# Six of a feed-forward block's first products taken from the stream not yet normalised, with eight PSUM banks in turn

## The chip, the cores and the metric

The kernel runs on one core of one Trainium2 chip. Its time is the device time of one execution in microseconds (us), lower is better; a kernel's figure is the median of its runs. TensorE does the matrix products into PSUM (8 banks of 512 float32 columns in each of 128 partitions), VectorE (DVE) and ScalarE (ACT) do the elementwise work, SyncE issues nearly all loads, GpSimd (POOL) a few subtractions.

## What is computed

The reference runs two stacks on 256 tokens of width 1024. The first (a conditioned block of attention with low-rank projections, short convolution and mixtures of experts) ends in an RMS norm. The change touches only the second stack, which is two layers of

```
x = layer_norm(ALPHA * x + 0.5 * swiglu_ffn(x, ffn1_w_gu, ffn1_w_down))
x = layer_norm(ALPHA * x + hybrid_mixer(x, w_in, w_out, ...))
x = layer_norm(ALPHA * x + 0.5 * swiglu_ffn(x, ffn2_w_gu, ffn2_w_down))

def swiglu_ffn(x, w_gu, w_down):
    a, u = split(x @ w_gu)          # 1024 -> 2 * 2816
    return (silu(a) * u) @ w_down   # 2816 -> 1024
```

All values are float32. The kernel gets float32 accuracy from fp32r products: a factor is split into a high part (rounded to fp32r) and a low part (the rest), and high*high + high*low + low*high are added up in PSUM.

## The kernel before

**Order of work.** Each engine runs its own program, written out stage by stage in Python; the order inside an engine is the order in which the methods `pe`, `act`, `dve`, `pool` of the stage classes issue instructions, and the engines meet through counting semaphores (`L.wait`, `L.inc`). Nothing reorders it. The stages of a layer are `ffns[0]`, `lns[0]`, `mixer`, `lns[1]`, `ffns[1]`, `lns[2]`, and two layers follow each other.

**Units of weight.** A feed-forward block (`Ffn`) first computes 22 pairs of 128 hidden features: unit 2f is the gate part, unit 2f+1 the linear part of pair f, and a unit is 128 columns of `w_gu` over all 8 tiles of 128 inputs. The weights of a unit are cast by ACT (`round_weights`, L2374, 128x1024) to the high part and subtracted by DVE (`split_weights`, L2379) to the low part, in one of `UNITS` = 4 buffers in `WS`; unit u can be cast only when unit u-4 has been multiplied (`units_used`). The loads from memory run ahead into `ring`.

**Two forms of a unit.** From unit `RAW_UNITS` = 4 on, `products` (L2398, L2403) multiplies the unit with the normalised stream, whose high and low parts lie in `XS`: 8 times a product of 512 columns (high weights with both parts of x) and one of 256. ACT then copies one half out of PSUM (`keep_low`, L2444) and DVE adds the other (`sum_parts`, L2503). The first four units are "raw" (`raw_products`, L587 to L589): they multiply the stream as it is before the norm is known, times the norm's gain (`RAW_HIGH`, `RAW_LOW`), 24 products of 260 or 256 columns. Once the norm's mean and reciprocal root are known, DVE corrects them in three steps (`correct_raw`, L595, L597, L600). DVE then forms silu(a)*u (L2525 or L2528) and splits it for the second matrix (`split_hidden`, L2510).

**The entries.** There are four places where a norm leads into a feed-forward block, and at each TensorE works on raw units while DVE and ACT finish the norm. Entry 1 is `norms[4]` (class `Norm`) into `ffns[0]` of the first layer; entries 2 and 4 are `lns[1]` (class `LayerNorm`, after the mixer) into `ffns[1]` of the first and second layer; entry 3 is `lns[2]` (class `EarlyLayerNorm`) into `ffns[0]` of the second layer. At entries 2 and 4 TensorE's order is unit 0, the sums of squares (`pe_sums`, L1034), a wait for the variance, units 1 to 3, then unit 4 as the pieces of `XS` appear (`stream_high` L780 on ACT, `stream_low` L784 on DVE). In `LayerNorm` ACT squares (L1056), casts unit 4, takes the root (L1060), then adds the bias (L1063) and casts to `XS` tile by tile; DVE subtracts the mean, splits units 2 and 3, adds epsilon to the variance (L1080), splits unit 4, takes the reciprocal (L1083), scales the tiles (L1086) and splits unit 5 last.

**PSUM.** Pairs f use banks 0/1, 2/3, 4/5 in turn (`bank`), so that unit u >= 6 waits until pair u//2-3 is finished (`hidden`). The norm's sums lie in banks 2 and 3 (`LayerNorm`) or 6 and 7.

## Time and profile before

| | |
|---|---|
| time, median of 3 runs | 2259.85 us (2259.22 to 2265.28) |
| the profiled execution: its time, its span | 2261.75 us, 2259.9 us |
| TensorE busy | 1980.1 us, 88% of the span |
| DVE busy, ACT busy | 1203.0 us (53%), 795.0 us (35%) |
| granted TensorE clock, mean | 0.955 of full speed |

The span runs from the first to the last instruction; the execution's time lies 1.85 us above it. The second stack begins at about 1222 us of the span. In the timeline a row is start, duration, engine, line, operation, output<-inputs, shapes and count; a bracket tells how long the engine sat idle and who released it. Matmul ends are modelled, so pace is read from start to start.

### The profile page before, as it was taken

Reading aid. Unit: us, or ns where it says so; the run is one execution under the profiler, and the core shown is the slowest. Engines: PE = TensorE matmul, PEld = TensorE weight load, DVE = VectorE, ACT = ScalarE, POOL = GpSimd, SP = SyncE. Lnnn points to the kernel's source line nnn. Section 1 sums busy time; section 2 is a strip of 40 time slices with the busy share of each in tenths; the row PEclk is TensorE's granted clock in tenths of the full one; section 3 lists DMA queues with packets and bytes.
Section 4 is the critical chain, followed back from the end, with each engine's and each line's share of the span. In section 5 each row is a group of like instructions: output and inputs, shape, how many; then the busy total and the mean of one; then the engine's idle time right before and its main releaser. Section 6 shows DMA issues by size and latency. Waiting matters only on the chain.

```text
span 2259.9 us, 45225 instructions
## 1 busy us (share of the span) xinstructions
PE 1980.1 (88%) x17666; PEld 1533.0 (68%) x17669; DVE 1203.0 (53%) x2486; ACT 795.0 (35%) x1535; POOL 28.3 (1%) x39
## 2 busy tenths in 40 slices
PE   7989887766779988766677999998999999998998
PEld 3557554434449855443445888987888888987887
DVE  3798322111227632111124766877767766877766
ACT  2233110000014411000003654555655654556554
POOL 0000000000000000000000000100001000100000
PEclk9999999888989999888898999999999999999999
DMA  9779999999997699999999645416656545416651
GB/s 409 299 320 392 429 431 431 432 431 431 431 431 301 253 393 431 432 432 432 431 432 400 219 145 184 161 48 214 203 150 221 177 149 179 162 49 223 203 150 59
DMA packets 238736, 660.83 MB, mean 292 GB/s; under 512 B 6416, under 2 KB 197920, under 8 KB 208672
## 3 DMA queue, kind: packets, MB, share of 16 engines
q1 hardware_dynamic: 238160, 657.25, 73.8%
q10 hardware_dynamic: 464, 2.05, 0.2%
q8 instruction: 75, 1.23, 0.2%
q14 instruction: 37, 0.30, 0.0%
HBM read 658.22 MB, written 1.06 MB: 292 GB/s over the span
## 4 chain that ended last, share of the span: by engine, by line
PE 60%; DMA 21%; DVE 11%; SPq 3%; issue 2%; ACT 2%; another core or an unknown queue 1%; PEld 0%; DVEq 0%; ACTq 0%; PEldq 0%
PE ps L2398 19%; PE ps L2403 10%; DMA A<-in_moe_w_up 8%; PE ps L1748 7%; DMA ring<-in_moe_w_up 6%; DMA arena<-in_moe_w_up 4%; PE ps L2730 3%; PE ps L1777 3%; SPq L3296 2%; DVE ring L546 2%; DMA ring<-in_ffn_w_gu 2%; PE ps L2886 2%; PE ps L1730 1%; PE ps L1698 1%; PE ps L2180 1%
## 5 line engine op out<-in xcount | busy, mean ns | idle before, releaser
L2398 PE MATMUL ps<-XS,WS 128*128 128x512 f32 x1280 | 449.8, 396 | 8.3 <-DVE WS L2379 8.2
L2379 DVE TENSOR_TENSOR WS<-ring,WS 128x1024 fp32r<-128x1024 f32 (+1 forms) x272 | 324.0, 1193 | 176.5 <-ACT WS L2374 176.0
L2374 ACT CAST WS<-ring 128x1024 fp32r<-128x1024 f32 (+1 forms) x272 | 278.3, 1024 | 275.8 <-PE ps L2403 258.9
L2403 PE MATMUL ps<-XS,WS 128*128 128x256 f32 x1280 | 357.9, 280 | 0.0
L2028 DVE TENSOR_TENSOR RS<-RS,ps 64x256 f32<-64x256 f32 x70 | 29.6, 423 | 577.7 <-ACT RS L1837 577.7
L1748 PE MATMUL ps<-ring,RS 128*32 128x256 f32 x2176 | 238.8, 451 | 87.2 <-DMA ring<-in_moe_w_up 32.6
L2398 PEld LDWEIGHTS ps<-XS,WS 128*128 128x128 f32 x1280 | 240.1, 188 | 68.1 <-issue 6.1
L2403 PEld LDWEIGHTS ps<-XS,WS 128*128 128x128 f32 x1280 | 241.4, 189 | 0.0
L1748 PEld LDWEIGHTS ps<-ring,RS 128*32 128x32 f32 x2176 | 127.2, 129 | 149.6 <-issue 128.8
L2398 PE MATMUL ps<-HS,WS 128*128 128x512 f32 x616 | 216.4, 396 | 0.0
L1748 PE MATMUL ps<-arena,RS 128*32 128x256 f32 x1120 | 168.3, 467 | 49.9 <-DMA A<-in_moe_w_up 24.9
L1837 ACT ACTIVATE RS<-ps 64x256 f32<-64x256 f32 x70 | 26.3, 375 | 487.8 <-PE ps L1748 487.8
L2403 PE MATMUL ps<-HS,WS 128*128 128x256 f32 x704 | 197.0, 280 | 0.0
L1748 PEld LDWEIGHTS ps<-arena,RS 128*32 128x32 f32 x1120 | 82.7, 134 | 86.8 <-issue 76.7
L2398 PEld LDWEIGHTS ps<-HS,WS 128*128 128x128 f32 x616 | 115.5, 188 | 27.3
L2403 PEld LDWEIGHTS ps<-HS,WS 128*128 128x128 f32 x704 | 133.0, 189 | 0.1
L1748 PE MATMUL ps<-SPARE,RS 128*32 128x256 f32 x576 | 81.5, 446 | 47.3 <-DMA arena<-in_moe_w_up 24.0
L1843 ACT COPY arena<-ps 128x256 f32<-128x256 f32 x70 | 26.0, 372 | 266.4 <-PE ps L1777 266.4
L546 DVE CUSTOM_DVE_ANT_0 ring<-ring,arena,VECS 128x1024 f32<-128x1024 f32 x80 | 98.8, 1280 | 4.8 <-DMA ring<-in_mod_later 4.7
L1748 PEld LDWEIGHTS ps<-SPARE,RS 128*32 128x32 f32 x576 | 45.1, 128 | 79.4 <-issue 68.2
L2034 DVE COPY arena<-ps 64x128 f32<-64x128 f32 x140 | 39.7, 283 | 105.4 <-PE ps L1764 103.2
L1748 PE MATMUL ps<-A,RS 128*32 128x256 f32 x608 | 85.9, 446 | 0.0
(410 smaller groups left out, 3526.7 us busy)
## 6 DMA issues: line engine op xcount, KB each, us to landing
ring<-in_ffn_w_gu SPq DMA_DIRECT2D x88, 1024.0 KB, 7.4
arena<-in_moe_w_down SPq DMA_DIRECT2D x32, 2048.0 KB, 48.7
ring<-in_moe_w_up SPq DMA_DIRECT2D x32, 2048.0 KB, 47.8
ring<-in_moe_w_down SPq DMA_DIRECT2D x32, 2048.0 KB, 47.7
ring<-in_moe_w_gate SPq DMA_DIRECT2D x32, 2048.0 KB, 46.5
ring<-in_ffn_w_down SPq DMA_DIRECT2D x32, 1408.0 KB, 6.4
ring<-in_mod_later SPq DMA_DIRECT2D x20, 2048.0 KB, 10.6
SPARE<-in_moe_w_gate SPq DMA_DIRECT2D x16, 2048.0 KB, 43.5
```

Of the source, the lines that this page charges most:

```text
L546: L.inc(L.eng.tensor_tensor_reduce(out=rows, in0=rows, in1=COND_ROW, scale=1.0, scalar=vcol("b_mod", 1, 48 * l + c), op0=ALU.mult, op1=ALU ...
L1748: mm = pe.matmul(ps[self.lane_rows(q), 0, 0:HALF_FF], x, weight, start=k == 0, stop=k == KD - 1)
L1777: mm = pe.matmul(ps[self.lane_rows(q), 7, 0:D // 4], self.HB[:, c, :], down[:, c, q * (D // 4):(q + 1) * (D // 4)], start=c == 0, stop=c = ...
L2028: v.tensor_tensor(self.H[0:2 * CAP], self.SG[2 * CAP:P], ps[2 * CAP:P, 0, 0:HALF_FF], ALU.mult)\
L2034: v.tensor_copy(self.HB[h * 2 * CAP:(h + 1) * 2 * CAP], turned[:, h]).then_inc(self.h_kept.sem, 1)
L2374: L.inc(L.eng.copy(self.parts(u)[0], source), self.w_high)
L2379: L.inc(L.eng.tensor_tensor(wl, self.unit(u)[1], high(wh), ALU.subtract), self.w_split)
L2398: L.eng.matmul(ps[:, bank, :].rearrange("p (j t) -> p j t", j=2), wh[:, i, :], moving[:, :, k, :], start=k == 0, stop=False)
L2403: mm = L.eng.matmul(ps[:, bank, 0:TL], wl[:, i, :], moving[:, 0, k, :], start=False, stop=k == total - 1)
L2730: mm = pe.matmul(out_ap, weights[:, k, :], XS[:, x, k, :], start=k == 0 and x == 0 and weights is high_part, stop=k == KD - 1 and weights ...
L2886: mm = pe.matmul(self.y_tile(m), weights[:, k - first, cols], YS[:, k, x, :], start=m % 2 == 0 and k == 0 and x == 0 and weights is high_part,
L3296: sp.dma_start(loads[at][0][0], src).then_inc(slot_in[place_of[at]].sem, 16)
```

## The change

Units 4 and 5 become raw as well (`RAW_UNITS` 6), so the stream of `XS` is first needed at unit 6. Eight banks are used in turn, beginning at bank 4 where a `LayerNorm` precedes; the wait for the variance moves from unit 2 to unit 6, and the wait for a finished pair now reaches back four pairs. The casts and splits of units 5, 6 and 7 move into the norm: unit 5 goes into its middle, units 6 and 7 to its end (they were done inside pair 1 of the feed-forward block). Units 4 and 5 need DVE's three correction steps instead of an ACT copy and one DVE addition.

In `LayerNorm` the cast of unit 5 stands ahead of ACT's wait for the variance, in `Norm` and `EarlyLayerNorm` behind the root.

```diff
--- before.py
+++ after.py
@@ -72,7 +72,7 @@
 UNITS = (RING - RING_2) * SLOT // (2 * UNIT)
 MIXER_UNITS = 4 * 5 + KD
 CONV_AHEAD = 2
-RAW_UNITS = 4
+RAW_UNITS = 6
 FFN_UNITS = 2 * FFT + KD * 3
 FIRST_BYTE = SCRATCH + 256
 
@@ -694,10 +694,12 @@
                                            bias=LNP[:, (2 * self.i + 1) * KD + k:(2 * self.i + 1) * KD + k + 1]), self.done)
                     if k and on:
                         stream_high(L, self.done, k - 1, self.split)
+                    if k == 3 and on and stage is ffns[0]:
+                        stage.round_weights(L, UNITS + 1, later)
                 if on:
                     stream_high(L, self.done, KD - 1, self.split)
-                    if self.raw:
-                        stage.round_weights(L, UNITS + 1, later)
+                    for u in (2, 3) if stage is ffns[0] else (1,):
+                        stage.round_weights(L, UNITS + u, later)
                 end(L, "act")
 
             def dve_first(self, L, k):
@@ -752,11 +754,13 @@
                         stream_low(L, k - 2, self.split)
                     if k == 3 and on and self.raw:
                         stage.split_weights(L, UNITS, later)
+                    if k == 6 and on and stage is ffns[0]:
+                        stage.split_weights(L, UNITS + 1, later)
                 if on:
                     for k in (KD - 2, KD - 1):
                         stream_low(L, k, self.split)
-                if on:
-                    stage.split_weights(L, UNITS + 1, later)
+                    for u in (2, 3) if stage is ffns[0] else (1,):
+                        stage.split_weights(L, UNITS + u, later)
                 end(L, "dve")
 
             def pool(self, L):
@@ -957,9 +961,11 @@
                         L.inc(L.eng.activation(CONV_XS[:, 0, k, :], A[:, k, 0:T], ACT.Identity, bias=self.shift(k)), conv.x_high)
                     conv.round_weights(L, CONV_AHEAD)
                 else:
+                    ffns[0].round_weights(L, UNITS + 1)
                     for k in range(KD):
                         stream_high(L, self.scaled, k, self.split)
-                    ffns[0].round_weights(L, UNITS + 1)
+                    for u in (UNITS + 2, UNITS + 3):
+                        ffns[0].round_weights(L, u)
                 end(L, "act")
 
             def dve(self, L):
@@ -988,6 +994,8 @@
                                                          op0=ALU.mult, op1=ALU.mult), self.scaled)
                         if k >= 2:
                             stream_low(L, k - 2, self.split)
+                        if k == 4:
+                            ffns[0].split_weights(L, UNITS + 1)
                 if self is norms[2]:
                     for k in range(KD):
                         L.eng.wait_ge(conv.x_high.sem, k + 1)
@@ -997,7 +1005,8 @@
                 if self.which == 2:
                     for k in (KD - 2, KD - 1):
                         stream_low(L, k, self.split)
-                    ffns[0].split_weights(L, UNITS + 1)
+                    for u in (UNITS + 2, UNITS + 3):
+                        ffns[0].split_weights(L, u)
                 end(L, "dve")
 
 
@@ -1055,7 +1064,8 @@
                     L.wait(self.centred, k + 1)
                     L.inc(L.eng.activation(LN_TILES[:, k, TL:TA], LN_TILES[:, k, 0:TL], ACT.Square), self.squares)
                 stage, later = self.next
-                stage.round_weights(L, UNITS, later)
+                for u in (UNITS, UNITS + 1):
+                    stage.round_weights(L, u, later)
                 L.wait(self.var, 1)
                 L.inc(L.eng.activation(RS[:, 0, 0:TL], RS[:, 0, 0:TL], ACT.Sqrt), self.std)
                 for k in range(KD):
@@ -1065,7 +1075,8 @@
                     if k:
                         stream_high(L, self.done, k - 1, self.split)
                 stream_high(L, self.done, KD - 1, self.split)
-                stage.round_weights(L, UNITS + 1, later)
+                for u in (UNITS + 2, UNITS + 3):
+                    stage.round_weights(L, u, later)
                 end(L, "act")
 
             def dve(self, L):
@@ -1073,12 +1084,12 @@
                 for k in range(KD):
                     L.inc(L.eng.tensor_tensor(LN_TILES[:, k, 0:TL], XT[:, k, 0:TL], LN_MEAN, ALU.subtract), self.centred)
                 stage, later = self.next
-                stage.split_weights(L, UNITS - 2, later)
-                stage.split_weights(L, UNITS - 1, later)
+                for u in (UNITS - 2, UNITS - 1, UNITS):
+                    stage.split_weights(L, u, later)
                 L.wait(self.sums, 1)
 
                 L.inc(L.eng.tensor_scalar(RS[:, 0, 0:TL], ps[:, self.banks[1], 0:TL], LN_EPS / ALPHA ** 2, None, ALU.add), self.var)
-                stage.split_weights(L, UNITS, later)
+                stage.split_weights(L, UNITS + 1, later)
                 L.wait(self.std, 1)
                 L.inc(L.eng.reciprocal(RS[:, 0, 0:TL], RS[:, 0, 0:TL]))
                 L.join()
@@ -1090,7 +1101,8 @@
                         stream_low(L, k - 2, self.split)
                 for k in (KD - 2, KD - 1):
                     stream_low(L, k, self.split)
-                stage.split_weights(L, UNITS + 1, later)
+                for u in (UNITS + 2, UNITS + 3):
+                    stage.split_weights(L, u, later)
                 end(L, "dve")
 
 
@@ -2380,7 +2392,7 @@
 
             def bank(self, u):
 
-                return 2 * (u // 2 % 3) + u % 2
+                return 2 * ((u // 2 + (2 if self.entry else 0)) % 4) + u % 2
 
             def pe(self, L):
 
@@ -2404,9 +2416,6 @@
                     L.inc(mm, self.w_used)
 
                 for u in range(RAW_UNITS):
-                    if u == 2 and self.entry:
-                        L.wait(self.entry.var, 1)
-                        L.wait(self.entry.mean_kept, 1)
                     raw_products(L, self, u, self.bank(u))
                     if u == 0 and self.entry:
                         self.entry.pe_sums(L)
@@ -2415,8 +2424,11 @@
                         L.eng.wait_ge(stages_done.sem, norms[4].before_sums)
                         L.eng.sem_inc(stages_done.sem, 1)
                 for u in range(RAW_UNITS, 2 * FFT):
-                    if u >= 6:
-                        L.wait(self.hidden, u // 2 - 2)
+                    if u == RAW_UNITS and self.entry:
+                        L.wait(self.entry.var, 1)
+                        L.wait(self.entry.mean_kept, 1)
+                    if u >= 8:
+                        L.wait(self.hidden, u // 2 - 3)
                     products(u, self.bank(u), XS)
                 L.wait(self.hidden, FFT - 1)
                 for m in range(KD):
@@ -2445,13 +2457,14 @@
 
                 for f in range(FFT):
                     raw = 2 * f < RAW_UNITS
-                    if f:
+                    if f > 1:
                         round_weights(UNITS + 2 * f)
                     if not raw:
                         L.wait(self.hidden, f - 1)
                         keep_low(2 * f, SA[f % 2], self.bank(2 * f), self.low_kept)
                     if f:
                         round_hidden(f - 1)
+                    if f > 1:
                         round_weights(UNITS + 2 * f + 1)
                     L.wait(self.summed, f + 1)
                     if raw:
@@ -2512,11 +2525,12 @@
                 for f in range(FFT):
                     raw = 2 * f < RAW_UNITS
                     part = correct if raw else sum_parts
-                    if f:
+                    if f > 1:
                         split_weights(UNITS + 2 * f)
                     part(2 * f, SA[f % 2], self.summed)
                     if f:
                         split_hidden(f - 1)
+                    if f > 1:
                         split_weights(UNITS + 2 * f + 1)
                     part(2 * f + 1, HF[f % 2])
                     L.wait(self.silu, f + 1)
```

**ACT inside `LayerNorm`, from the squares (L1056, now L1065) to the second tile of the scaled stream.** `WS` is the weight buffer, `RS` holds the root; the waits are `split_used` (an earlier unit has been multiplied), `norm_var` (variance ready), `norm_scaled` (a tile scaled by DVE). Before:

```order
L1056 ACTIVATE arena<-arena 128x256 [waits ln_centred] x8
L2374 CAST WS<-ring 128x1024 [waits split_used,slot_in2]
L1060 ACTIVATE RS<-RS 128x256 [waits norm_var]
L1063 ACTIVATE XT<-XT,LNP 128x256 [waits norm_scaled] x2
L780 CAST XS<-XT 128x256 [waits norm_done]
```

Now:

```order
L1065 ACTIVATE arena<-arena 128x256 [waits ln_centred] x8
L2386 CAST WS<-ring 128x1024 [waits split_used,slot_in2] x2
L1070 ACTIVATE RS<-RS 128x256 [waits norm_var]
L1073 ACTIVATE XT<-XT,LNP 128x256 [waits norm_scaled] x2
L784 CAST XS<-XT 128x256 [waits norm_done]
```

There are two casts (units 4 and 5) ahead of the root where there was one.

**DVE inside `LayerNorm`, from the centring (L1074, now L1085) to the reciprocal.** L1080 (now L1091) reads the sum of squares, L2379 (now L2391) is a split. Before:

```order
L1074 TENSOR_TENSOR arena<-XT,RS 128x256 x7
L2379 TENSOR_TENSOR WS<-ring,WS 128x1024 [waits split_high] x2
L1080 TENSOR_SCALAR RS<-ps 128x256 [waits norm_sums]
L2379 TENSOR_TENSOR WS<-ring,WS 128x1024 [waits split_high]
L1083 RECIPROCAL RS<-RS 128x256 [waits norm_std]
```

Now:

```order
L1085 TENSOR_TENSOR arena<-XT,RS 128x256 x7
L2391 TENSOR_TENSOR WS<-ring,WS 128x1024 [waits split_high] x3
L1091 TENSOR_SCALAR RS<-ps 128x256 [waits norm_sums]
L2391 TENSOR_TENSOR WS<-ring,WS 128x1024 [waits split_high]
L1094 RECIPROCAL RS<-RS 128x256 [waits norm_std]
```

Unit 4 is split ahead of the variance, and unit 5 in the place that unit 4 had.

**DVE at the start of the feed-forward block, from the first product with silu (L2525, now L2539) to the split of unit 8.** L595, L597 and L600 are one correction, L2510 (now L2523) is `split_hidden`. Before:

```order
L2525 SCALAR_TENSOR_TENSOR arena<-arena,SPARE 128x256 [waits loop_line_dve,ffn_silu]
L2379 TENSOR_TENSOR WS<-ring,WS 128x1024 [waits split_high]
L595 TENSOR_REDUCE SPARE<-ps 128x2 [waits split_used]
L597 SCALAR_TENSOR_TENSOR arena<-RS,SPARE,ps 128x256 [waits loop_line_dve]
L600 TENSOR_TENSOR arena<-arena,RS 128x256 [waits loop_line_dve]
L2510 TENSOR_TENSOR HS<-arena,HS 128x256 [waits ffn_h_high]
L2379 TENSOR_TENSOR WS<-ring,WS 128x1024 [waits split_high]
L595 TENSOR_REDUCE SPARE<-ps 128x2 [waits split_used]
L597 SCALAR_TENSOR_TENSOR arena<-RS,SPARE,ps 128x256 [waits loop_line_dve]
L600 TENSOR_TENSOR arena<-arena,RS 128x256 [waits loop_line_dve]
L2525 SCALAR_TENSOR_TENSOR arena<-arena,SPARE 128x256 [waits loop_line_dve,ffn_silu]
L2379 TENSOR_TENSOR WS<-ring,WS 128x1024 [waits split_high]
```

Now:

```order
L2539 SCALAR_TENSOR_TENSOR arena<-arena,SPARE 128x256 [waits loop_line_dve,ffn_silu]
L595 TENSOR_REDUCE SPARE<-ps 128x2 [waits split_used]
L597 SCALAR_TENSOR_TENSOR arena<-RS,SPARE,ps 128x256 [waits loop_line_dve]
L600 TENSOR_TENSOR arena<-arena,RS 128x256 [waits loop_line_dve]
L2523 TENSOR_TENSOR HS<-arena,HS 128x256 [waits ffn_h_high]
L595 TENSOR_REDUCE SPARE<-ps 128x2 [waits split_used]
L597 SCALAR_TENSOR_TENSOR arena<-RS,SPARE,ps 128x256 [waits loop_line_dve]
L600 TENSOR_TENSOR arena<-arena,RS 128x256 [waits loop_line_dve]
L2539 SCALAR_TENSOR_TENSOR arena<-arena,SPARE 128x256 [waits loop_line_dve,ffn_silu]
L2391 TENSOR_TENSOR WS<-ring,WS 128x1024 [waits split_high]
```

The splits of units 6 and 7 are gone from between the corrections; they stand, with nothing between them, at the norm's end, where the split of unit 5 stood. The split of unit 8 closes the same list of DVE work in both.

## Rows read from the trace of the kernel before

**Rows 1.** The page: span, and busy time of each engine.

```profile
span 2259.9 us, 45225 instructions
PE 1980.1 (88%) x17666; PEld 1533.0 (68%) x17669; DVE 1203.0 (53%) x2486; ACT 795.0 (35%) x1535; POOL 28.3 (1%) x39
```

**Rows 2.** Waits of TensorE, 1225 to 2260: total us, times, longest.

```profile
PE ps L2398 <- DVE WS L2379: 8.2, 7, 1.5
```

**Rows 3.** Timeline of TensorE at entry 2: units 0, 1, 5, 6, 8.

```profile
1550.05 0.28 PE L589 MATMUL ps<-RAW_HIGH,WS 128*128 128x260 f32 x1
...
1556.35 0.28 PE L589 MATMUL ps<-RAW_HIGH,WS 128*128 128x260 f32 x1
...
1566.45 0.50 PE L2398 MATMUL ps<-XS,WS 128*128 128x512 f32 x1 [1.09 <-DVE WS L2379]
...
1570.61 0.47 PE L2398 MATMUL ps<-XS,WS 128*128 128x512 f32 x1 [1.11 <-DVE WS L2379]
...
1576.23 0.39 PE L2398 MATMUL ps<-XS,WS 128*128 128x512 f32 x1
```

**Rows 4.** Timeline of DVE at entry 2: splits, reciprocal, first corrections.

```profile
1554.16 1.22 DVE L2379 TENSOR_TENSOR WS<-ring,WS 128x1024 fp32r<-128x1024 f32 x1
1555.29 1.75 DVE L1083 RECIPROCAL RS<-RS 128x256 f32<-128x256 f32 x1
...
1565.17 1.23 DVE L2379 TENSOR_TENSOR WS<-ring,WS 128x1024 fp32r<-128x1024 f32 x1 [0.49 <-ACT WS L2374]
1566.54 0.16 DVE L595 TENSOR_REDUCE SPARE<-ps 128x2 f32<-128x4 f32 x1
...
1569.24 1.22 DVE L2379 TENSOR_TENSOR WS<-ring,WS 128x1024 fp32r<-128x1024 f32 x1
...
1571.76 1.22 DVE L2379 TENSOR_TENSOR WS<-ring,WS 128x1024 fp32r<-128x1024 f32 x1
...
1574.54 1.22 DVE L2379 TENSOR_TENSOR WS<-ring,WS 128x1024 fp32r<-128x1024 f32 x1
```

**Rows 5.** Timeline of ACT at entry 2: casts of units 4 and 5, the root.

```profile
1550.42 1.05 ACT L2374 CAST WS<-ring 128x1024 fp32r<-128x1024 f32 x1 [0.71 <-PE ps L589]
1554.28 0.42 ACT L1060 ACTIVATE RS<-RS 128x256 f32<-128x256 f32 x1 [2.81 <-DVE RS L1080]
...
1564.10 1.04 ACT L2374 CAST WS<-ring 128x1024 fp32r<-128x1024 f32 x1
```

**Rows 6.** Timeline of DVE and TensorE at entry 1: unit 8 split, unit 8 begun.

```profile
1254.75 1.22 DVE L2379 TENSOR_TENSOR WS<-ring,WS 128x1024 fp32r<-128x1024 f32 x1
...
1256.55 0.40 PE L2398 MATMUL ps<-XS,WS 128*128 128x512 f32 x1
```

**Rows 7.** The same of entry 3.

```profile
1764.69 1.22 DVE L2379 TENSOR_TENSOR WS<-ring,WS 128x1024 fp32r<-128x1024 f32 x1
...
1766.49 0.40 PE L2398 MATMUL ps<-XS,WS 128*128 128x512 f32 x1
```

**Rows 8.** Timeline at entry 4: reciprocal, unit 1's last product, unit 8.

```profile
2063.87 1.75 DVE L1083 RECIPROCAL RS<-RS 128x256 f32<-128x256 f32 x1
...
2064.93 0.28 PE L589 MATMUL ps<-RAW_HIGH,WS 128*128 128x260 f32 x1
...
2083.11 1.22 DVE L2379 TENSOR_TENSOR WS<-ring,WS 128x1024 fp32r<-128x1024 f32 x1
...
2084.81 0.39 PE L2398 MATMUL ps<-XS,WS 128*128 128x512 f32 x1
```

**Rows 9.** Windows: length, busy PE, PEld, DVE, ACT, POOL, granted clock, DMA.

```profile
1542.00:1544.00 2.00, 1.13 (x4) 0.68 (x4) 1.42 (x4) 1.76 (x3) 0.00 (x0) 1.00 1.09 386
1544.00:1546.00 2.00, 1.68 (x4) 0.90 (x4) 1.15 (x3) 1.19 (x4) 0.00 (x0) 0.68 0.96 341
1546.00:1548.00 2.00, 1.55 (x8) 1.53 (x8) 1.51 (x5) 1.42 (x5) 0.00 (x0) 0.50 0.04 16
...
1568.00:1570.00 2.00, 1.50 (x9) 1.05 (x8) 1.85 (x4) 1.80 (x4) 0.00 (x0) 1.00 0.00 0
...
2054.00:2056.00 2.00, 1.31 (x5) 0.89 (x6) 1.26 (x4) 1.44 (x4) 0.00 (x0) 1.00 0.96 341
```

More of the change, by code:

```diff
@@ L152 @@
 ACT_PER_LAYER = 7
-DVE_PER_LAYER = 172
-DVE_LAST = 169
+DVE_PER_LAYER = 180
+DVE_LAST = 177
 SPLITS_PER_LAYER = 2 * FFN_UNITS + MIXER_UNITS
```

## The prediction

> **What bounds the kernel now.** I read the page first. TensorE is busy for 1980.1 of 2259.9 us [rows 1], and in the second stack nearly without a break, so a change there can only give back what TensorE waits for. The waits of TensorE say how much that is: for a split of weight units 5 to 7 it sat idle 7 times, 8.2 us in total and never over 1.5 us at once [rows 2]. Each of these lies at one of the four entries, one at entry 1 and two at each of the others. That is the whole purse: 8.2 us of 2259.9, or 0.36%. About 0.3% is what a measurement of this kernel can tell from no change.
>
> The timelines of one entry say why it waits there. At entry 2 TensorE begins unit 6 at 1570.61 after 1.11 us of idleness, released by DVE's split that began at 1569.24 [rows 3, 4]. From the start of a split to the first product of its unit is 1570.61 - 1569.24 = 1.37 us. DVE itself hardly rests between the reciprocal at 1555.29 and the split of unit 8 at 1574.54 [rows 4]. So at the entries DVE's list of work is the bound. By unit 8 it is no longer: the split at 1574.54 would let unit 8 begin at 1575.91, and TensorE comes only at 1576.23 [rows 3, 4], 0.32 late. That slack is the same kind at the other entries: 1254.75 + 1.37 = 1256.12 against 1256.55, so 0.43 [rows 6]; 1764.69 + 1.37 against 1766.49, 0.43 [rows 7]; 2083.11 + 1.37 against 2084.81, 0.33 [rows 8].
>
> **The change part by part.** *Raw units 4 and 5 on TensorE* cost nothing: by their columns a raw unit (8 times 260 + 256 + 260) is 1% more than a unit on `XS` (8 times 512 + 256), and units 6 and 7 need (1576.23 - 1570.61) / 2 = 2.81 us each from start to start [rows 3], so a raw one 2.84. What is won is that they need no `XS`, so TensorE can run them while the norm ends.
>
> *The splits of units 6 and 7* move ahead of the first two pairs' corrections. TensorE then doesn't wait for them behind corrections; it waits for unit 8 instead. This is the step that decides the sum. Ahead of the split of unit 8 DVE has the same list as before: the splits up to unit 7, the corrections of units 0 to 3, two products with silu, one split of hidden values. Only the order within the list differs, as the excerpt of DVE's order shows. So unit 8 can't be split earlier than before unless DVE's idle time shrinks. Then each entry gains no more than its slack, as TensorE, now ahead of time, takes unit 8 as soon as it is split. At entries 1 and 3 I take just that: -0.43 and -0.43. The inner split of unit 5 there (behind the third or fifth tile of the stream) delays the rest of the stream by one split, 1555.29 - 1554.16 = 1.13 us [rows 4], which is the split that vanished from the end.
>
> *The cast of unit 5 ahead of the root* (entries 2 and 4) is what adds a wait. It needs unit 1 to have been multiplied. TensorE starts unit 1 only behind the sums of squares; its last product begins at 1556.35 [rows 3]. After unit 0 the cast began 1550.42 - 1550.05 = 0.37 later [rows 3, 5], so unit 5 is cast from 1556.72. ACT's root stood at 1554.28 [rows 5] and is now behind it. DVE's split of unit 5 follows its cast by 1565.17 - 1564.10 = 1.07 [rows 4, 5], so from 1557.79, and it too stands ahead of the reciprocal, which comes 1.13 later: 1558.92 instead of 1555.29. The norm is 3.63 late. Entry 4 gives the same: unit 1's last product at 2064.93 puts the reciprocal at 2064.93 + 0.37 + 1.07 + 1.13 = 2067.50, against 2063.87, again 3.63 [rows 8]. Queued behind are the scaling of eight tiles, their casts, the casts and splits of units 6 and 7 and all corrections. One split (1.13) of the list has been done inside the delay, so unit 8 is split 3.63 - 1.13 = 2.50 later than before; less the slack, TensorE begins it 2.18 late at entry 2 and 2.17 at entry 4.
>
> What TensorE sees at entry 2: units 2 to 5 follow unit 1 without a break, 1556.35 + 4 x 2.84 = about 1567.8; unit 6 can be split at 1564.10 + 3.63 + 1.07 = 1568.80 and begins at 1570.17, after 2.3 us of waiting; unit 8 begins at 1576.23 + 2.18 = 1578.41, after another 2.6. Two waits of 1.1 idle have become two of over 2.
>
> The trace shows first that a ready root can stand behind a cast: at 1550.42 ACT sat 0.71 for TensorE with its next work queued behind [rows 5]. The Trainium skill, "TensorE: Matmul & The Clock Gate", section "Architectural detail: the array is 16× 32×32, not 1× 128×128", calls the queues of ScalarE and VectorE strictly first in, first out, which speaks against this change; by it the two entries lose 2.2 us each, and if either engine could pass the waiting pair they would gain their slack. The trace agrees so far as the one wait of 0.71 shows.
>
> *Eight banks and the later waits* cost nothing and give nothing. The wait for a pair four back instead of three would matter if TensorE waited for finished pairs; among its waits from 1225 on, only the splits of units and the edges of the mixer appear, and the former make 8.2 us [rows 2]. The wait for the variance moves to unit 6, which needs the finished stream anyway. If that cover were gone it would be the same moment: the stream needs the root.
>
> *Two more corrections per entry* on DVE (units 4 and 5) replace two ACT copies and two DVE additions. Behind the split of unit 8 the splits must now come every 2.81. A split, a correction, a split of hidden values and the next split take 1571.76 - 1569.24 = 2.52; a split, a correction, a product with silu and the next split 1574.54 - 1571.76 = 2.78 [rows 4]. So unit 9 is ready 0.29 ahead of TensorE and unit 10 0.32 ahead: no new wait, but the cover is thin. Without it each unit costs what it lacks; I take zero, at most 0.5 per entry.
>
> *Sum*: -0.43 + 2.18 - 0.43 + 2.17 = +3.5 us. It stands against the profiled execution, 2261.75 with a span of 2259.9; that lies 1.9 above the median of 2259.85, so I carry the difference over: 2259.85 + 3.5 = **2263.3 us**, 0.15% slower, which a measurement calls no change.
>
> **The rivals.** *The clock falls in the new waits* (slower side of the same mechanism). At entry 2 the trace has a stretch in which TensorE worked 1.13 and 1.68 of 2 us, and the granted clock fell to 0.68 and then 0.50, the level of 1.2 GHz [rows 9]; the like stretch at entry 4 kept 1.00 with 1.31 of 2 busy, and so did the present waits at 1.50 of 2 [rows 9]. With two waits of over 2 us around one unit the new stretch has about as little work as the one that fell. The fall in the rows cost 1.68 x 0.32 + 1.55 x 0.50 = 1.3 us of TensorE's busy time, and a whole unit at half pace would cost 2.8; I take 1.7, nearer to the row. One fall gives 2265, three give 2268.4. For it: idle shares like those before the fall. Against: DVE still bounds unit 8, so slow units 6 and 7 would be hidden. The Trainium skill, same page, section "A second HAM failure mode: psum-queue depth-cycling", says that short idle times between groups of matmuls can make the clock swing between its two levels; by that page entries 2 and 4 would fall each time, about 2266.7 by the price above. The trace has both outcomes for like stretches. Chance 0.25.
>
> *The block at entries 2 and 4 doesn't bite* (other side). If the cast of unit 5 is ready before the root (unit 1 done sooner, or the sums later), the reciprocal stays, and all four entries gain their slack: -0.43 - 0.32 - 0.43 - 0.33 = -1.5, 2258.3. The point that decides is whether unit 1 ends before the variance; now it ends 2.1 us behind the root's start (1556.35 against 1554.28) [rows 3, 5], and nothing in the change moves it forward. Chance 0.12.
>
> *The waits vanish as meant*: if DVE has reserve that I don't see and unit 8 comes early too, up to 8.2 us of idleness goes [rows 2], 2251.7, the only way to faster by over 0.3%. DVE's nearly unbroken row from 1555.29 to 1574.54 speaks against it [rows 4]. Chance 0.05.
>
> *DVE falls behind in pairs 2 and 3*: 0.5 per entry on top, 2265.3. Chance 0.08. My forecast as it stands: 0.50.
>
> **How the numbers follow.** Within the forecast the handovers may each be off by some tenths, 2261.5 to 2265.1. The range takes in the rival without the block at its lower end and two or three falls of the clock at its upper: 2257.5 to 2269.5; the full success and many falls stay out. Faster by over 0.3% (below 2253.1) is the vanishing alone, 0.05. Slower by over 0.3% (above 2266.6) needs two falls or a fall with DVE behind: most of the clock's 0.25 and some of the rest of the cases, less what is hidden, 0.19. That leaves 0.76 within 0.3%.
>
> **What would show it.** Right: at entries 2 and 4 ACT's root starts about 3.4 us later, behind a cast that waited for TensorE; the reciprocal 3.6 later; TensorE waits over 2 us before unit 6 and again before unit 8; at entries 1 and 3 a wait before unit 8 alone, and unit 8 0.4 nearer to the entry's start. Wrong: a reciprocal in its old place, unit 8 reached without a wait, waits from unit 9 on, or a granted clock under 1.00 behind an entry.

## The result, and the profile after

The changed kernel takes 2265.03 us (median of 20 runs, 2261.74 to 2270.72), the kernel before in the same comparison 2262.10 us (20 runs, 2258.50 to 2265.85). The ratio is **1.0018, 95% interval 1.0011 to 1.0024**: slower by 0.18%, which is within the 0.3% that counts as no change. On the first median of before the ratio gives 2259.85 x 1.0018 = 2263.9 us; the prediction was 2263.3.

The page of the profiled execution (2261.74 us) shows almost no difference to before [rows 1]:

```profile
span 2259.8 us, 45345 instructions
PE 1979.7 (88%) x17730; PEld 1540.8 (68%) x17733; DVE 1207.8 (53%) x2502; ACT 793.1 (35%) x1527; POOL 28.3 (1%) x39
```

The waits of TensorE from 1225 us on answer to [rows 2]: total us, times, longest.

```profile
PE ps L2410 <- DVE WS L2391: 9.4, 6, 2.6
```

Seven waits of at most 1.5 us became six of up to 2.6, and the total grew by 1.2. The timeline of ACT at entry 2 (answers to [rows 5]) shows the first cause:

```profile
1547.49 1.05 ACT L2386 CAST WS<-ring 128x1024 fp32r<-128x1024 f32 x1
1553.79 1.05 ACT L2386 CAST WS<-ring 128x1024 fp32r<-128x1024 f32 x1 [5.25 <-PE ps L589]
1554.74 0.41 ACT L1070 ACTIVATE RS<-RS 128x256 f32<-128x256 f32 x1
```

ACT sits idle for 5.25 us before it casts unit 5, and the root stands behind it; the variance that the root needs is ready 3.43 us before the root begins (1551.31, next rows, to 1554.74). The timeline of DVE at the same entry (answers to [rows 4]):

```profile
1546.99 3.49 DVE L2391 TENSOR_TENSOR WS<-ring,WS 128x1024 fp32r<-128x1024 f32 x3
1550.89 0.42 DVE L1091 TENSOR_SCALAR RS<-ps 128x256 f32<-128x256 f32 x1 [0.41 <-PE ps L1043]
1554.87 1.23 DVE L2391 TENSOR_TENSOR WS<-ring,WS 128x1024 fp32r<-128x1024 f32 x1 [3.56 <-ACT WS L2386]
1556.01 1.75 DVE L1094 RECIPROCAL RS<-RS 128x256 f32<-128x256 f32 x1
...
1565.89 2.36 DVE L2391 TENSOR_TENSOR WS<-ring,WS 128x1024 fp32r<-128x1024 f32 x2 [0.49 <-ACT WS L2386]
1568.40 0.16 DVE L595 TENSOR_REDUCE SPARE<-ps 128x2 f32<-128x4 f32 x1
...
1574.12 1.22 DVE L2391 TENSOR_TENSOR WS<-ring,WS 128x1024 fp32r<-128x1024 f32 x1
```

The variance is ready at 1551.31, and DVE then waits 3.56 us for the cast of unit 5. From there on its row is as full as before: the splits of units 6 and 7 in one piece at 1565.89, the corrections, and the split of unit 8 at 1574.12. TensorE at entry 2 (timeline; answers to [rows 3]): the last product of unit 1, then the first products of units 6 and 8:

```profile
1553.42 0.28 PE L589 MATMUL ps<-RAW_HIGH,WS 128*128 128x260 f32 x1
...
1567.38 0.47 PE L2410 MATMUL ps<-XS,WS 128*128 128x512 f32 x1 [2.27 <-DVE WS L2391]
...
1575.49 0.47 PE L2410 MATMUL ps<-XS,WS 128*128 128x512 f32 x1 [0.71 <-DVE WS L2391]
```

The measure used from here on is the time from the start of unit 1's last product to the start of unit 8's first: here 1575.49 - 1553.42 = 22.07 us. Before it was 1576.23 - 1556.35 = 19.88 [rows 3].

| kernel | entry 1 | entry 2 | entry 3 | entry 4 |
|---|---|---|---|---|
| before | 18.95 | 19.88 | 20.45 | 19.88 |
| the change | 18.18 | 22.07 | 20.02 | 22.07 |
| difference | -0.77 | +2.19 | -0.43 | +2.19 |

The sum is +3.2 us. A second loss lies behind unit 8 at entry 3. Windows at entry 2 (units 6 and 7) and at entry 3 (around the start of unit 8): length, busy PE, PEld, DVE, ACT, POOL, granted clock, DMA share and GB/s; and the first product of unit 8 at entry 3 from TensorE's timeline.

```profile
1568.00:1570.00 2.00, 2.00 (x9) 1.69 (x8) 1.75 (x6) 0.62 (x2) 0.00 (x0) 0.68 0.26 53
1570.00:1572.00 2.00, 2.00 (x8) 1.70 (x7) 1.78 (x6) 0.49 (x2) 0.00 (x0) 0.50 1.06 363
...
1762.00:1764.00 2.00, 0.78 (x5) 0.41 (x3) 1.83 (x6) 1.44 (x2) 0.00 (x0) 1.00 0.96 294
1764.00:1766.00 2.00, 0.60 (x3) 0.59 (x4) 1.93 (x5) 1.35 (x2) 0.00 (x0) 1.00 0.84 295
1766.00:1768.00 2.00, 2.00 (x9) 1.71 (x9) 1.97 (x5) 1.67 (x3) 0.00 (x0) 0.67 0.10 35
1768.00:1770.00 2.00, 2.00 (x7) 1.64 (x7) 1.86 (x4) 0.61 (x3) 0.00 (x0) 0.50 0.00 0
```

```profile
1765.40 0.47 PE L2410 MATMUL ps<-XS,WS 128*128 128x512 f32 x1 [2.62 <-DVE WS L2391]
```

At entry 3 TensorE idled 2.62 us before unit 8 (begun at 1765.40), and then the granted clock fell to 0.67 and to 0.50, the 1.2 GHz level. From unit 8 to unit 20 it took 34.95 us instead of the 33.36 of entries 2 and 4: +1.6 us. At entries 2 and 4 the clock fell too, on units 6 and 7, but there nothing was lost by it (below). So by these two profiles the change costs 3.2 + 1.6 = 4.8 us of some 2262, or 0.21%; measured 0.18%.

That the two profiled executions nonetheless took the same 2261.7 us lies in other places. Unit 1 of entry 1 ends 0.9 us earlier in the one of after (at 1236.70; in the change's control, experiment 9, at 1238.28). The stretch up to unit 1 of entry 2 is 1.3 us shorter, which is the fall of the clock that before had there [rows 9]: its unit 0 took 3.55 us from its first product to its last instead of 2.81, and it began 0.6 us later behind the last products ahead of it. From the last unit of entry 3's block to the first product of entry 4 it is 0.7 shorter (189.68 instead of 190.40; the control of before has 189.66), and the block behind entry 3 ran at the faster of two paces (last section), some 1.9.

### The profile page after: what moved, and what is told of

Its sections match the earlier page's. It is cut to its first block, busy times and chain, and to the rows that moved or that the text cites. A ratio compares the mean times of both kernels' runs of the same rounds, so it can differ in the third digit from the quotient of the medians.

```text
span 2259.8 us, 45345 instructions
## 1 busy us (share of the span) xinstructions
PE 1979.7 (88%) x17730; PEld 1540.8 (68%) x17733; DVE 1207.8 (53%) x2502; ACT 793.1 (35%) x1527; POOL 28.3 (1%) x39
## 3 DMA queue, kind: packets, MB, share of 16 engines
HBM read 658.22 MB, written 1.06 MB: 292 GB/s over the span
## 4 chain that ended last, share of the span: by engine, by line
PE 63%; DMA 21%; DVE 10%; issue 2%; ACT 2%; SPq 1%; another core or an unknown queue 1%; DVEq 0%; ACTq 0%; PEldq 0%
PE ps L2410 18%; DMA A<-in_moe_w_up 12%; PE ps L2415 10%; PE ps L1760 8%; DMA ring<-in_moe_w_up 6%; PE ps L2744 3%; PE ps L1789 3%; DVE ring L546 2%; DMA arena<-in_moe_w_up 2%; PE ps L2900 2%; PE ps L1742 1%; SPq L3310 1%; PE ps L1710 1%; PE ps L2192 1%; PE ps L2194 1%
## 5 line engine op out<-in xcount | busy, mean ns | idle before, releaser
L2410 PE MATMUL ps<-XS,WS 128*128 128x512 f32 x1216 | 429.1, 397 | 9.4 <-DVE WS L2391 9.4
L2391 DVE TENSOR_TENSOR WS<-ring,WS 128x1024 fp32r<-128x1024 f32 (+1 forms) x272 | 323.6, 1193 | 175.1 <-ACT WS L2386 174.7
L2415 PE MATMUL ps<-XS,WS 128*128 128x256 f32 x1216 | 342.9, 282 | 0.0
L2410 PEld LDWEIGHTS ps<-XS,WS 128*128 128x128 f32 x1216 | 230.0, 189 | 63.5 <-issue 11.0
L2415 PEld LDWEIGHTS ps<-XS,WS 128*128 128x128 f32 x1216 | 232.0, 191 | 0.0
```

The source lines that it names most:

```text
L2391: L.inc(L.eng.tensor_tensor(wl, self.unit(u)[1], high(wh), ALU.subtract), self.w_split)
L2410: L.eng.matmul(ps[:, bank, :].rearrange("p (j t) -> p j t", j=2), wh[:, i, :], moving[:, :, k, :], start=k == 0, stop=False)
L2415: mm = L.eng.matmul(ps[:, bank, 0:TL], wl[:, i, :], moving[:, 0, k, :], start=False, stop=k == total - 1)
```

## The experiments

**Theory:** what decides is where unit 5's cast and split stand at entries 2 and 4, and DVE's list ahead of unit 8 everywhere. **Rivals:** the eight banks or the later waits matter; only one of the two engines holds the norm up; the clock's fall costs most of it. Ratios are to the kernel before on the same chip. "The entries" are the four numbers of the table above.

**1. Eight banks and the moved waits alone**, on the kernel before (whose wait for the variance stands ahead of unit 2, behind unit 1).

```diff
-                return 2 * (u // 2 % 3) + u % 2
+                return 2 * ((u // 2 + (2 if self.entry else 0)) % 4) + u % 2
...
-                    if u == 2 and self.entry:
-                        L.wait(self.entry.var, 1)
-                        L.wait(self.entry.mean_kept, 1)
...
-                    if u >= 6:
-                        L.wait(self.hidden, u // 2 - 2)
+                    if u == 6 and self.entry:
+                        L.wait(self.entry.var, 1)
+                        L.wait(self.entry.mean_kept, 1)
+                    if u >= 8:
+                        L.wait(self.hidden, u // 2 - 3)
```

> The kernel before, with the banks of the change alone: eight banks in turn from bank 4 at the later entries, the wait for the variance at unit 6, the wait for a finished pair four back. Theory: nothing waited for a bank, so the places of all units stay within 0.1 us of the kernel before and the ratio is 1.000 within 0.0006. Rival (PSUM banks set a part of the time): TensorE's waits before units 6 and 7 shrink, or the pace of the units from 8 on changes, ratio 0.997 to 0.999; or, if the banks that the norm's sums use collide, over 1.001.

Measured: 1.0009 (0.9999 to 1.0020); entries 18.52, 19.89, 20.29, 19.89. Entries 2 and 4 stay to 0.01 us, so the banks give nothing there. Two numbers miss a little: entries 1 and 3 came 0.43 and 0.16 earlier, where 0.1 was expected, and the ratio lies 0.0003 above the expected band. Entry 1 moves as much without any edit to it (below, on the slack); for entry 3 one profile doesn't tell.

**2. The hold-up alone**, on the kernel before: its unit 5 is cast ahead of the root and split ahead of the reciprocal, unit 4 is split ahead of the variance; `RAW_UNITS` stays 4. The cast and split that stood at the norm's end are gone.

```diff
-                stage.round_weights(L, UNITS, later)
+                for u in (UNITS, UNITS + 1):
+                    stage.round_weights(L, u, later)
                 L.wait(self.var, 1)
...
-                stage.split_weights(L, UNITS, later)
+                stage.split_weights(L, UNITS + 1, later)
                 L.wait(self.std, 1)
...
```

> The kernel before, with only the hold-up in LayerNorm added: unit 5 is cast ahead of the root and split ahead of the reciprocal, unit 4 is split ahead of the variance; four raw units, six banks, no more corrections, units 6 and 7 split where they were. Theory: the reciprocal is 3.6 us late at entries 2 and 4, and unit 8 begins about 1.8 us later at each (the split of unit 5 no longer stands at the end); entries 1 and 3 untouched; total +3.7 us, ratio 1.0010 to 1.0022. Rival A (the loss of the change comes from the corrections, the banks or the raw units): ratio 1.000 within 0.0005. If the loss is mostly from falls of the clock behind the waits: the units begin where the theory says, but the time is lost behind them at a granted clock of 0.5.

Measured: 1.0013 (1.0003 to 1.0022); entries 19.06, 21.90, 20.36, 21.91. Entries 2 and 4 lose 2.0 us each, entries 1 and 3 move by 0.1. This one edit makes nearly all of the change's loss at entries 2 and 4 (2.19 us each).

**3. Without the hold-up:** the change, but cast and split of unit 5 inside `LayerNorm`'s tile loops.

```diff
-                for u in (UNITS, UNITS + 1):
-                    stage.round_weights(L, u, later)
+                stage.round_weights(L, UNITS, later)
...
+                    if k == 3:
+                        stage.round_weights(L, UNITS + 1, later)
...
-                stage.split_weights(L, UNITS + 1, later)
                 L.wait(self.std, 1)
...
+                    if k == 6:
+                        stage.split_weights(L, UNITS + 1, later)
```

> The change, with one thing taken back in LayerNorm: unit 5 is cast behind the root, inside ACT's loop over the tiles, and split inside DVE's loop, as EarlyLayerNorm has it. Theory (the cast and split of unit 5 hold up the norm at entries 2 and 4, and DVE's list bounds unit 8 everywhere): the reciprocal follows the variance without a wait for a cast; from unit 1's last product to unit 8 it takes about 19 us instead of 22.07, so 2.9 to 3.0 us less than in the change at each of entries 2 and 4; entries 1 and 3 stay as in the change. Total about 6 us under the change and 2 to 3 us under the kernel before: ratio to before 0.9987 to 0.9992. Rival A (the loss is the two more corrections on DVE or the clock, not the block): entries 2 and 4 stay near 22 us, ratio near 1.0015. Rival B (the raw units themselves are slower): ratio over 1.000 even with the norm on time.

Measured: 1.0008 (0.9999 to 1.0017); entries 18.13, 19.69, 19.97, 19.70. The 2.2 us of entries 2 and 4 are gone, but a miss in two numbers: they came back to the place of before (19.88) less 0.2, not to 19.0, and the ratio isn't below 1. Against before the entries give -1.7 us in all, a ratio of 0.9993; why it came out above is not settled (last section). A ratio over 1.000 with the norm on time is what rival B forecast, but its cause isn't there: the raw units follow each other every 2.85 us in the kernel before, in the change and here. So a clean change gains next to nothing: DVE's list bounds unit 8 (experiments 6 to 8).

**4 and 5. Which of the two engines holds it up.** In the one, only ACT's cast moves behind the root; in the other, only DVE's split moves into the loop. Each has one execution alone (2261.24 and 2269.73 us), from which no ratio follows; the entries tell.

```diff
-                for u in (UNITS, UNITS + 1):
-                    stage.round_weights(L, u, later)
+                stage.round_weights(L, UNITS, later)
                 L.wait(self.var, 1)
                 L.inc(L.eng.activation(RS[:, 0, 0:TL], RS[:, 0, 0:TL], ACT.Sqrt), self.std)
+                stage.round_weights(L, UNITS + 1, later)
```

> The change, with only ACT's half of the hold-up taken back: in LayerNorm unit 5 is cast right behind the root, but DVE still splits it ahead of the reciprocal. Theory (each engine's order alone holds the norm): the root starts at once behind the variance, but the reciprocal still waits for the cast by way of the split, so from unit 1's last product to the reciprocal's start 2.6 us as in the change (1556.01 - 1553.42), and to unit 8 22.07 us within 0.2. Rival (it is ACT's order alone that holds it): the reciprocal comes under 1.3 us behind the root's end and unit 8 about 2.4 us earlier, as in the kernel with both moved (19.69).

```diff
-                stage.split_weights(L, UNITS + 1, later)
                 L.wait(self.std, 1)
...
+                    if k == 6:
+                        stage.split_weights(L, UNITS + 1, later)
```

> The change, with only DVE's half taken back: in LayerNorm DVE splits unit 5 inside the loop over the tiles, ACT still casts it ahead of the root. Theory: the root stays behind the cast (0.4 + 0.95 us after unit 1's last product begins), the reciprocal follows the root and starts 0.75 us earlier than in the change, but the split of unit 5 is back in DVE's list behind it: from unit 1's last product to unit 8 22.07 - 0.75 + 1.13 = 22.4 us. Rival (DVE's order alone holds it): 19.7 us.

Measured, with the cast moved: entries 18.65, 22.07, 20.03, 22.08. ACT's timeline at entry 2:

```profile
1548.31 0.42 ACT L1069 ACTIVATE RS<-RS 128x256 f32<-128x256 f32 x1 [2.81 <-DVE RS L1091]
1550.75 1.05 ACT L2386 CAST WS<-ring 128x1024 fp32r<-128x1024 f32 x1 [2.03 <-PE ps L589]
```

and DVE's:

```profile
1551.83 1.23 DVE L2391 TENSOR_TENSOR WS<-ring,WS 128x1024 fp32r<-128x1024 f32 x1 [3.56 <-ACT WS L2386]
1552.97 1.75 DVE L1094 RECIPROCAL RS<-RS 128x256 f32<-128x256 f32 x1
```

The root is done at 1548.73, yet the reciprocal comes at 1552.97: the split alone holds it. With the split moved: entries 18.61, 22.39, 20.02, 22.39. ACT's timeline:

```profile
1551.99 1.05 ACT L2387 CAST WS<-ring 128x1024 fp32r<-128x1024 f32 x1 [5.25 <-PE ps L589]
1552.94 0.41 ACT L1070 ACTIVATE RS<-RS 128x256 f32<-128x256 f32 x1
```

Now the cast alone holds it. Either one alone costs the whole price; mending one of them mends nothing. (With the split moved the reciprocal does come earlier, 1.77 instead of 2.59 us behind unit 1's last product, but the split of unit 5 is back in DVE's list behind it.)

**6. A shorter list at entry 1**, on the kernel of experiment 3. The norm before entry 1 subtracts no mean, so the three-step correction is one multiplication there (silu and the product after it leave out the mean's term as well).

```diff
+            if light:
+                L.inc(L.eng.tensor_tensor(o, ps[:, bank, 0:TL], RS[:, 0, 0:TL], ALU.mult), signal)
+                return
             L.inc(L.eng.tensor_reduce(WEIGHT_SUMS[:, u, :], ps[:, bank, TL:TL + 4].rearrange("p (a h) -> p a h", h=2), X, ALU.add))
```

> The first kernel of this call, and at entry 1 alone the corrections of the six raw units in one step instead of three: the norm there has no mean and no bias, so the first two steps add zeros. This takes 12 DVE instructions, 4 x (0.2 + 0.5) = 2.8 us of them ahead of the split of unit 8, out of DVE's list at entry 1. Theory (DVE's list bounds unit 8): the wait before unit 8 at entry 1, 1.0 us in the change, goes completely; unit 8 begins 1.0 to 1.1 us nearer to unit 1 than in the change (21.10 us there, 20.0 here), and the rest as in the first kernel; ratio to before 0.9982 to 0.9988. Rival (TensorE waits there for something else: a bank, a cast, a load): the wait before unit 8 stays.

Measured: 1.0005 (0.9995 to 1.0015); entries 17.17, 19.70, 20.01, 19.69. Taking work off DVE's list ahead of unit 8 takes away the wait before it, at that entry alone: 18.13 to 17.17. That the list is the bound there is shown. The ratio is a miss: 0.9982 to 0.9988 was expected. Against before the entries give -2.6 us, and at entry 3 the clock fell behind the wait (from unit 8 to unit 20 35.50 us), which it didn't in experiment 3 (33.99), so the profile accounts for some -1.1 us, a ratio of 0.9995; the rest is not settled (last section).

**7. The order of the list**, on the kernel of experiment 3: units 8 to 11 are cast and split one pair earlier, among the corrections instead of behind them.

```diff
-                    if f > 1:
-                        split_weights(UNITS + 2 * f)
+                    if f in (1, 2):
+                        split_weights(UNITS + 2 * f + 2)
+                    elif f > 3:
+                        split_weights(UNITS + 2 * f)
```

(and the same for odd units and for ACT's casts)

> The change with unit 5 cast and split inside the loops of LayerNorm (the first kernel of the first call), and with the casts and splits of units 8 to 11 done one pair of hidden features earlier on ACT and DVE: units 8 and 9 beside the corrections of pair 1, units 10 and 11 beside those of pair 2, nothing in pair 3. Nothing is added or left out. Theory (DVE's list ahead of the split of unit 8 is what TensorE waits for): 3.0 us of corrections and products leave the list ahead of unit 8, so the waits before unit 8 (1.0, 2.4, 2.6, 2.4 us in that kernel) go; from unit 1's last product to unit 8 about 17.2, 17.4, 17.4, 17.4 us at the four entries, against 18.95, 19.88, 20.45, 19.88 in the kernel before; no new wait up to unit 12; total 9 us under the kernel before at equal pace of the later units, ratio 0.995 to 0.997. Rival A (TensorE then waits for a finished pair or for the cast of unit 9 or 10): the waits move to units 9 to 12 and less than half of that is won, ratio 0.998 to 1.000. Rival B (the pace of a whole block, 2.77 or 2.83 us a unit, moves the time by more than the entries do): the entries are as the theory says and the ratio is nearer to 1 all the same.

Measured: **0.9978 (0.9966 to 0.9989)**, 2254.83 us; entries 17.17, 17.33, 17.34, 17.31. No wait is left before unit 8. The ratio misses the expected 0.995 to 0.997 by a little. Small new waits stand before unit 12 at entries 2 to 4, where the lead is given back (total us, times, longest):

```profile
PE ps L2412 <- DVE WS L2393: 2.1, 3, 0.9
```

**8. The lead kept longer**, for pairs 1 to 9 (`f in (1, 2)` becomes `0 < f < 10`, `f > 3` becomes `f > 10`).

> The kernel with both steps of unit 5 inside the loops and units 8 to 11 rounded and split one pair earlier, with the one-pair lead kept for pairs 1 to 9 instead of 1 and 2 (pair 10 gives it back). If VectorE's order alone is what made TensorE wait 0.75 to 1.05 us ahead of unit 12 at entries 2 to 4, these waits go (2.1 us in all), the entries stay at 17.2 to 17.4 us from unit 1 to unit 8, and the ratio to the kernel before is 0.9965 to 0.9980. Rival: the lead only moves the shortage to pair 10, where a wait of about the same size appears ahead of unit 28, or the finished pairs come out later and hold a bank; then the ratio is no better than that of the shorter lead, 0.9978 or above.

Measured: **0.9963 (0.9950 to 0.9976), 2252.38 us** (6 runs), faster than both kernels; entries 17.17, 17.30, 17.32, 17.30. In TensorE's waits from 1225 us on no row of a weight split is left; the largest are now

```profile
PE ps L1035 <- DVE XT L3224: 5.9, 8, 1.2
PE ps L587 <- DVE RAW_LOW L577: 3.5, 3, 2.5
```

which before had too (5.9 and 3.7 us in all). The ratio is a shade better than the expected 0.9965 to 0.9980. DVE at entry 2 of this kernel (timeline), from the splits of units 6 and 7:

```profile
1563.54 2.36 DVE L2393 TENSOR_TENSOR WS<-ring,WS 128x1024 fp32r<-128x1024 f32 x2 [0.50 <-ACT WS L2388]
...
1568.74 1.22 DVE L2393 TENSOR_TENSOR WS<-ring,WS 128x1024 fp32r<-128x1024 f32 x1
1569.88 0.16 DVE L595 TENSOR_REDUCE SPARE<-ps 128x2 f32<-128x4 f32 x1
...
1571.27 1.22 DVE L2393 TENSOR_TENSOR WS<-ring,WS 128x1024 fp32r<-128x1024 f32 x1
```

Unit 8 is split 1568.74 - 1563.54 = 5.20 us after unit 6, where the change needs 1574.12 - 1565.89 = 8.23: two corrections, a product and a split of hidden values now stand behind it.

**9. Controls:** both kernels once more, unchanged.

> The kernel before once more, as a control. Theory: ratio 1.000 within its interval, which tells what a comparison in this call can tell apart; the entries repeat (from unit 1's last product to unit 8 18.95, 19.88, 20.45, 19.88 us within 0.3). The pace of the later units, 2.77 or 2.83 us from start to start over a whole block, which differed between blocks and kernels so far: if it belongs to the kernel, the blocks show 2.83, 2.77, 2.83, 2.77 again; if it is drawn anew in every execution, another pattern, and the span moves with it by about 2 us a block.

> The changed kernel once more, unchanged. What its order sets must come again: from the start of unit 1's last product to unit 8's start 18.2 to 18.7 us at entry 1, 22.07 at entries 2 and 4, 20.0 at entry 3, within 0.1 us at entries 2 to 4; ratio to the kernel before 1.0010 to 1.0025. If the two paces of a block belong to the execution and not to the kernel, the pattern over the four blocks need not be that of the first profile (2.83, 2.77, 2.77, 2.77); if they belonged to the order of the instructions, it must be the same. The fall of the granted clock behind unit 8 at entry 3 may come again (unit 8 about 4.2 us, unit 9 about 3.0) or not (2.8 each).

Measured: the kernel before 1.0003 (0.9990 to 1.0016), entries 18.91, 19.98, 20.35, 19.89. The change 1.0023 (1.0010 to 1.0037), entries 18.17, 22.06, 20.00, 22.07, and the clock fell again at entries 2 to 4 (unit 8 of entry 3 4.42 us; to unit 20 35.51 instead of 33.99).

## Why the prediction was right

- **The hold-up at entries 2 and 4** (forecast +2.18 and +2.17): measured +2.19 and +2.19. The steps hold one by one. The reciprocal was to come 0.37 + 1.07 + 1.13 = 2.57 us behind unit 1's last product; it came at 1556.01 - 1553.42 = 2.59, where before it stood 1.06 ahead of it [rows 3, 4]. Experiment 2 shows it alone, experiments 4 and 5 show that both engines hold. The Trainium skill's rule that ScalarE and VectorE work first in, first out ("TensorE: Matmul & The Clock Gate", section "Architectural detail: the array is 16× 32×32, not 1× 128×128") agrees with it on both engines: in the change a ready root stood 3.43 us behind a waiting cast, in experiment 4 a ready reciprocal 4.24 us (1548.73 to 1552.97) behind a waiting split. The row that the prediction took as a first sign of this, ACT's 0.71 us at 1550.42 [rows 5], didn't show it: the root wasn't ready then and came only behind 2.81 us more of waiting for the variance.
- **The slack at entries 1 and 3** (forecast -0.43 each): -0.43 at entry 3; -0.77 at entry 1, a term off by 0.34. There the start of the measure moved, not only its end. Reciprocals of entry 1 in before and in the change, and the change's unit 8:

```profile
1236.81 1.75 DVE L979 RECIPROCAL RS<-RS 128x256 f32<-128x256 f32 x1
...
1235.64 1.75 DVE L985 RECIPROCAL RS<-RS 128x256 f32<-128x256 f32 x1
1254.88 0.47 PE L2410 MATMUL ps<-XS,WS 128*128 128x512 f32 x1 [0.84 <-DVE WS L2391]
```

The reciprocal stands 0.79 us ahead of unit 1's last product in before and 1.06 in the change, where unit 0, at a granted clock of 0.50 for most of it in both, took 5.74 us instead of 5.27. From the reciprocal to unit 8 the entry went from 1256.55 - 1236.81 = 19.74 to 19.24 us: -0.50, near the forecast. Executions differ in this: the 18.65 of experiment 4 is 19.25 counted from the reciprocal, and in experiment 1, with four raw units, the reciprocal also stands 1.06 ahead.
- **Eight banks, moved waits:** nothing, as forecast (experiment 1). **Two more corrections:** no wait from unit 9 on, as forecast.
- **The sum:** forecast +3.5 us, the entries +3.2. The ratio of 1.0018 makes +4.1 of 2262; with the clock's 1.6 at entry 3 the trace accounts for 4.8, inside the interval (2.5 to 5.4). That 2263.3 and 2263.9 lie only 0.6 us apart is luck in part: the forecast left out the fall at entry 3, and the pace of a single block (last section) moves an execution by 1.9 us.
- **The clock, the first rival,** came in part. At entries 2 and 4 the forecast had two waits over 2 us; the second was 0.71, because the clock fell on units 6 and 7 (1567.38 to 1575.49 is 8.1 us, or 7.4 without the wait, for what took 5.6 before) and so used up the rest of what the wait would have been. This sign of being right didn't come, and one of being wrong did, a granted clock under 1.00 behind an entry. As the prediction said against this rival, DVE bounds unit 8, and the fall costs nothing: 22.07 at both. What it didn't place is entry 3, where the fall comes behind the wait and is paid in full. The price is as it took it: 1.7 forecast, 1.5 to 1.6 measured. The section of the Trainium skill that the prediction weighs ("TensorE: Matmul & The Clock Gate", "A second HAM failure mode: psum-queue depth-cycling"), which has short idle times make the clock swing, would by the prediction's reading have it fall at entries 2 and 4 each time: it did at both in both profiles of the change, but cost nothing there.
- **The rival "the waits vanish as meant"** was right to name 2251.7, and right to be refused for this order of DVE's work. Experiment 8 comes out there (2259.85 x 0.9963 = 2251.5) without taking any work off DVE. The purse of 8.2 us was counted too small: it holds the idle rows alone, but from start to start the entries of before lie 10.1 us in all above those of experiment 8. The ratio of experiment 8 makes 8.4, with an interval of 5.4 to 11.3, so it doesn't tell the two apart.

## What to carry to other kernels

Work put into an idle place of an engine's program must not wait for something later than what stands behind it: here a cast that waited for a product of TensorE, and a split that waited for the cast, held a finished norm for 3.6 us, and either alone still cost each entry 2.2 us or more. When a wait of the busiest engine is filled with work that another engine must then finish, look at that engine's list: what stands ahead of the next piece decided whether unit 8 came in time. Taking work out (experiment 6) and only moving it behind (experiments 7 and 8) both ended the wait. A wait just before a stretch that TensorE itself bounds can cost twice, in idle time and in the clock behind it (1.5 to 1.6 us here); the same fall ahead of a later wait cost nothing.

## What was not expected

**Two paces of the same products.** From unit 10 on (in experiment 7 from unit 13 on) the units of a block run at a constant pace, but that is one of two values. The first products of units 20 and 40 at entry 1 and at entry 2 in the profile of the change:

```profile
1288.87 0.40 PE L2410 MATMUL ps<-XS,WS 128*128 128x512 f32 x1
...
1345.40 0.40 PE L2410 MATMUL ps<-XS,WS 128*128 128x512 f32 x1
...
1608.84 0.39 PE L2410 MATMUL ps<-XS,WS 128*128 128x512 f32 x1
...
1664.31 0.39 PE L2410 MATMUL ps<-XS,WS 128*128 128x512 f32 x1
```

Twenty units take 56.53 us in the one and 55.47 in the other, 2.83 and 2.77 each, and the windows between show TensorE always busy at a granted clock of 1.00 in both:

```profile
1300.00:1340.00 40.00, 40.00 (x228) 34.63 (x228) 27.55 (x44) 22.72 (x42) 0.00 (x0) 1.00 0.46 141
1620.00:1660.00 40.00, 40.00 (x232) 35.28 (x232) 27.53 (x44) 23.72 (x44) 0.00 (x0) 1.00 0.47 146
```

Over the 36 units from unit 8 on that is 36 x 0.053 = 1.9 us a block, so up to 7.6 us an execution, more than the change is worth. The order of the instructions alone doesn't set it: the pattern over the four blocks was slow, fast, slow, fast in the first profile of before and slow, slow, fast, fast in its control; slow, fast, fast, fast in the change and fast, slow, slow, slow in its control. Experiment 1 had four fast blocks (span 2252.3 us) with a ratio of 1.0009 over its runs: one profile alone would have called it a gain. What sets the pace is open; the waits may have to do with it. In the nine stretches in which TensorE ran on from its raw units without a wait in its rows (the block of entry 1 in experiment 6, all four in experiment 8, units 8 to 11 at all four entries in experiment 7) the pace was the slow one; behind a wait both paces came. In experiment 7 it changed within a block: at entry 1 from 2.83 to 2.77 at unit 12, with no wait in the rows there. The profiled execution of experiment 8, with four slow blocks, was the longest of its six (2255.45 us, the shortest 2249.32). The kernels with six raw units had 21 slow blocks of 32, those with four 6 of 16. If that were more than chance it would be some 2.1 us an execution, of the size by which experiments 3 and 7 fell short of what their entries give (0.0015 and 0.0010 of the ratio, 3.4 and 2.2 us, in experiment 7 after the 2.8 us lost from start to start at unit 12); so few blocks don't tell.

**The clock's fall is not a matter of the wait alone.** With a wait of 2.5 to 2.6 us before unit 8 at entry 3 it fell in five of six profiles (not in experiment 3, with 2.52 us). After the waits of 2.27 us before unit 6 at entries 2 and 4 (the change, its control, experiment 4) it fell in all six cases, and after those of 2.2 to 2.3 us before unit 8 there (experiments 3, 5 and 6) in one of six (experiment 5, entry 4: from unit 8 to unit 20 35.45 us instead of 33.99). What else decides was not tried.
